# Second attention's entrance and lap in another order, final product by tile, weight splits in two halves

## The chip, the cores and the metric

One core of a Trainium2 chip runs the whole program in one launch. The time is that of the device for one execution, in microseconds (us). TensorE (PE) multiplies, VectorE (DVE), ScalarE (ACT) and GpSimd (POOL) work on elements, and SP issues the DMAs.

## The reference, cut to what matters

512 tokens of width 1024 pass through two blocks of two layers each, all in float32.

- First block, each layer: an RMS norm, three branches (a gated MLP with mixing over 128-token chunks, a retention branch, a gated delta rule), gates, an output product, and a sum onto x. After both layers there is a final norm.
- Second block, each layer: `h = rmsnorm(x)`, then a mixer with 8 self heads (latent attention in the first layer, grouped-query attention with rotary in the second), beside an attention with 4 heads over 256 memory tokens. Then:

```python
mem_out = _memory_attention(q_mem, mem_n, w_mem_kv[i], memq_norm[i], memk_norm[i])
x = x + jnp.concatenate([mix, mem_out], axis=-1) @ w_out[i]
x = x + _swiglu(_rmsnorm(x, norm_ffn[i]), w_gate_up[i], w_down[i])
```

Queries and keys get an RMS norm for each head (and rotary in the self heads) before `softmax(q k^T * scale) v`. The hidden width of the SwiGLU is 2816, that is 22 tiles of 128.

## The kernel before, in words

**Data.** x lies feature-major, xT[128, 8, 512]: eight tiles of 128 features by 512 tokens. Each engine has its own program, written out by hand, and semaphores join them (a wait names a count).

**Weights.** They come as 384 granules of 128x1024 float32 (512 KB) through four slots. For each granule SP loads `raw` (L753); ScalarE casts it to the high part `wh` (`hi2`, L1902, and its like at L1671, L1855, L2216), which waits for `loaded` and for `granule_done`; GpSimd subtracts, `wl = raw - wh` (`split`, L2263 and L2264), and counts `lo_ready`. TensorE waits for `lo_ready` and does three products for each tile (`three`, L822 to L824): high by high, high by low, low by high. Activations are split the same way: for the norm's output `ht` (a ring of four), VectorE scales (`scale_x`, L2924), ScalarE casts `hh` (`scaled_hi`, L1927), GpSimd subtracts `hl` (`scaled_lo`, L2396). `cast(name, parts)` in the attention casts the granules that lie four further on in the slots of those of `name`: "mk" fills those of mv, "mv" those of qm, "qm" of kv, "kv" of qA, "qA" of qB, and "qB" the first four of w_out.

**The second block's attention.** Products come in the order mk, mv (the memory's keys and values, from the split memory tokens mh and ml), then qm, kv, qA, qB from h. While mk and mv are multiplied, the norm of x is made: `square_b` (ScalarE, L1935), `add_b` (VectorE, L2931), and the sum on TensorE behind mv. `attention_block(i)` of each engine holds its own list. Then come steps of heads. Phase 0 has four memory heads, phase 1 eight self heads; each head has four steps, one for each 128 queries, and each phase a few more for what trails. In a step TensorE does QK of one tile (L1482 for the memory, L1487), transposes an earlier P (L1505), and every fourth step PV (L1523). VectorE finds the maximum (L3107) and the bias (L3109), ScalarE the exponential (L2198), VectorE the reciprocal (L3128) and scales P (L3130). The transposed P is copied to mPT, PT or PT_odd by ScalarE (L2187) and VectorE (L3119), the output by ScalarE to mixh (L2206) and by VectorE to mixl (L3136).

`attention_order(i, phases)` (L442) gives the order of steps. In the second attention (i = 1) both phases are one list: the last four steps of phase 0, (0,16) to (0,19), alternate with the first four of phase 1. Between steps each engine has a hook. There ScalarE squares the query tiles of qB (L1983 to L1995), takes roots (L2014), copies the turned queries (`feature`, L2030) and casts granules; VectorE ropes tiles (L2950, L2953, L2957), finishes reciprocals (`finish`, L2847) and does `square_sums` (L2900); TensorE turns query tiles feature-major (`turn_one`, L1338), those of qA at (0,4) to (0,7), those of qB at (1,4) to (1,7) (`late_turns`, L1441). In the phase 1 steps near its end `mixer_early` begins w_out.

**SwiGLU.** 44 granules of up and gate, then 22 of down (`down`, L1595 to L1612). Each down granule is multiplied into all eight output tiles, kt by kt, eight PSUM banks at once. After the last one VectorE adds the eight tiles onto xT in DOWN_ORDER = 4, 5, 6, 7, 0, 1, 2, 3 (L3157), and behind each add of the last layer SP stores the tile (256 KB, L814).

**The first block.** The same granules and splits. VectorE's steps named in the text: gmlp's product y (L2585), retention's rope sum (L2605) and its normalisation (L2634), the convolution (L2701). GpSimd also scales tokens (`scale_tokens`, L2415).

## Time and profile before

| | us |
|---|---|
| median of 3 runs (lowest to highest) | 2765.1 (2763.65 to 2766.12) |
| the profiled execution, its own time | 2765.28 |
| its span | 2763.2 |
| busy: PE | 2666.6 (97%) |
| busy: POOL | 1295.4 (47%) |
| busy: DVE | 1150.4 (42%) |
| busy: ACT | 1140.9 (41%) |
| share of the chain that ended last: PE, DVE, issue, POOL | 83%, 9%, 4%, 2% |

The span is what the profiler recorded of one execution; the 2.1 us between it and that execution's own time lie around the recorded instructions. Busy time says how full an engine is over all stages; it does not say which engine a stage waits for. The waits and the timelines do. A line number such as L2264 is that of the kernel; names such as wl<-raw,wh are the output and the inputs; in brackets stands how long the engine was idle before and what released it. Where a group has "x4", its time is that of four instructions together.

### The profile page before, as it was taken

The numbers are of one execution on the slowest core, as the hardware profiler recorded it, in microseconds if no ns is written. First come the engines' busy times: TensorE is split into PE (matmuls) and PEld (weight loads), VectorE is DVE, ScalarE is ACT, GpSimd is POOL, SyncE is SP. The second block draws the span as 40 slices with busy tenths as digits, with TensorE's granted clock in tenths as the row PEclk, the third lists the DMA queues.
The fourth block names the chain that finished last, engine by engine and source line by source line (L and its number), as shares of the span: only waits on it lengthen the run. The fifth ranks groups of instructions, "written<-read, shape, count | busy, mean of one in ns | idle before, by whom it ended". The sixth has DMA issues, their size and how long they took to land.

```text
span 2763.2 us, 37205 instructions
## 1 busy us (share of the span) xinstructions
PE 2666.6 (97%) x13032; PEld 2162.6 (78%) x13032; DVE 1150.4 (42%) x2191; ACT 1140.9 (41%) x1731; POOL 1295.4 (47%) x672
## 2 busy tenths in 40 slices
PE   7999999999999999999999999999999979999998
PEld 6768898888876888888887648888887746888887
DVE  4677643224477764322466562211104466221100
ACT  5427444323543744432445643333215454333321
POOL 5313565556631366555664213555547311365542
PEclk9999999999999999999999999999999999999999
DMA  4212101233221210133332002333333200233232
GB/s 173 84 45 70 46 26 40 96 99 130 87 79 44 69 40 31 47 99 93 120 115 69 24 31 71 98 98 98 99 109 107 82 31 16 84 106 99 91 99 69
DMA packets 62348, 215.07 MB, mean 78 GB/s; under 512 B 7296, under 2 KB 10496, under 8 KB 61824
## 3 DMA queue, kind: packets, MB, share of 16 engines
q1 hardware_dynamic: 62208, 213.28, 24.5%
q8 instruction: 79, 1.29, 0.2%
q14 instruction: 61, 0.50, 0.1%
HBM read 211.16 MB, written 2.10 MB: 77 GB/s over the span
## 4 chain that ended last, share of the span: by engine, by line
PE 83%; DVE 9%; issue 4%; POOL 2%; ACT 1%; DMA 0%; DVEq 0%; POOLq 0%; SPq 0%; ACTq 0%
PE bank L822 21%; PE bank L824 21%; PE bank L823 20%; PE pair L1523 3%; PE pair L822 2%; PE pair L824 2%; PE pair L823 2%; PE bank L1505 1%; PE bank L989 1%; PE bank L1484 1%; PE bank L1485 1%; DVE pair L2687 1%; DVE prod L2686 1%; PE pair L1338 1%; POOL EG L2341 1%
## 5 line engine op out<-in xcount | busy, mean ns | idle before, releaser
L2264 POOL TENSOR_TENSOR wl<-raw,wh 128x1024 fp32r<-128x1024 f32 x384 | 946.9, 2470 | 1281.7 <-ACT wh L1902 407.8
L822 PE MATMUL bank<-hh,wh 128*128 128x512 f32 x1536 | 607.4, 395 | 3.7 <-DVE y L2774 2.3
L824 PE MATMUL bank<-hh,wl 128*128 128x512 f32 x1536 | 599.2, 390 | 0.0
L823 PE MATMUL bank<-hl,wh 128*128 128x512 f32 x1536 | 598.9, 390 | 0.0
L822 PEld LDWEIGHTS bank<-hh,wh 128*128 128x128 f32 x1536 | 289.3, 188 | 66.2 <-issue 5.5
L823 PEld LDWEIGHTS bank<-hl,wh 128*128 128x128 f32 x1536 | 289.3, 188 | 61.9 <-issue 2.9
L824 PEld LDWEIGHTS bank<-hh,wl 128*128 128x128 f32 x1536 | 288.9, 188 | 60.9
L2216 ACT CAST wh<-raw 128x1024 fp32r<-128x1024 f32 x120 | 125.5, 1048 | 254.0 <-PE pair L824 140.2
L822 PE MATMUL bank<-wh,hh 128*128 128x512 f32 (+2 forms) x352 | 140.7, 400 | 13.1 <-POOL wl L2264 12.5
L1902 ACT CAST wh<-raw 128x1024 fp32r<-128x1024 f32 x84 | 86.7, 1048 | 125.2 <-PE bank L824 105.8
L824 PE MATMUL bank<-wh,hl 128*128 128x512 f32 (+2 forms) x352 | 135.1, 384 | 0.0
L823 PE MATMUL bank<-wl,hh 128*128 128x512 f32 (+2 forms) x352 | 135.0, 383 | 0.0
L2787 DVE TENSOR_TENSOR gs<-gs,bank 128x512 f32<-128x512 f32 x24 | 16.4, 684 | 275.3 <-PE bank L824 275.3
L1671 ACT CAST wh<-raw 128x1024 fp32r<-128x1024 f32 x104 | 108.9, 1049 | 42.7 <-DMA raw<-stream 18.5
L3150 DVE TENSOR_TENSOR at<-row,bank 128x512 f32<-128x512 f32 x44 | 30.3, 688 | 202.2 <-PE bank L824 199.4
L1855 ACT CAST wh<-raw 128x1024 fp32r<-128x1024 f32 x72 | 75.2, 1045 | 85.5 <-PE pair L824 43.8
L822 PE MATMUL bank<-ah,wh 128*128 (+1 forms) x264 | 102.7, 389 | 0.0
L823 PE MATMUL bank<-al,wh 128*128 (+1 forms) x264 | 102.7, 389 | 0.0
L824 PE MATMUL bank<-ah,wl 128*128 (+1 forms) x264 | 102.7, 389 | 0.0
L3147 DVE TENSOR_TENSOR at<-row,bank 128x512 f32<-128x512 f32 x44 | 30.3, 688 | 162.3 <-PE bank L824 161.6
L1871 ACT ACTIVATE gs<-bank 128x512 f32<-128x512 f32 x48 | 28.8, 600 | 166.5 <-PE bank L824 166.5
L822 PEld LDWEIGHTS bank<-wh,hh 128*128 128x128 f32 x352 | 67.8, 193 | 25.4 <-issue 13.8
(462 smaller groups left out, 5314.3 us busy)
## 6 DMA issues: line engine op xcount, KB each, us to landing
raw<-stream SPq DMA_DIRECT2D x384, 512.0 KB, 3.6
mraw<-memin SPq DMA_DIRECT2D x3, 1024.0 KB, 5.6
par<-params SPq DMA_DIRECT2D x2, 1124.5 KB, 9.0
out<-xT SPq DMA_DIRECT2D x8, 256.0 KB, 2.4
con<-consts SPq DMA_DIRECT2D x1, 1540.0 KB, 15.6
xT<-xin SPq DMA_DIRECT2D x1, 1536.0 KB, 8.5
xT<-xin SPq DMA_DIRECT2D x1, 512.0 KB, 3.9
con<-consts SPq DMA_DIRECT2D x1, 512.0 KB, 3.1
```

The lines of the kernel that those rows point to most:

```text
L822: mm(o, ah, bh, start=start, stop=False)
L823: mm(o, ah, bl, start=False, stop=False)
L824: return mm(o, al, bh, start=False, stop=stop)
L1523: x = mm(bk[value_bank(i, phase, a)], vv, pts[a % 2][kb][:, :], start=(kb == 0), stop=(kb == nk - 1))
L1671: nc.scalar.copy(wh[g % SLOTS][:, :], raw[g % SLOTS][:, :]).then_inc(hi_ready, 1)
L1855: nc.scalar.copy(wh[g % SLOTS][:, :], raw[g % SLOTS][:, :]).then_inc(hi_ready, 1)
L1871: A(gs[e][:, :], bk[e], ACT.Sigmoid).then_inc(s["gate_taken"].sem, 1)
L1902: nc.scalar.copy(wh[g % SLOTS][:, :], raw[g % SLOTS][:, :]).then_inc(hi_ready, 1)
L2216: nc.scalar.copy(wh[slot][:, :], raw[slot][:, :]).then_inc(hi_ready, 1)
L2264: return TT(wl[slot][:, :], raw[slot][:, :], wh[slot][:, :].bitcast(F32), ALU.subtract)
L3147: V.tensor_tensor(at_[j][:, :], row[:, :], bk[2 * j], ALU.mult).then_inc(t["f_gate"].sem, 1)
L3150: V.tensor_tensor(at_[j][:, :], row[:, :], bk[2 * j + 1], ALU.mult).then_inc(t["f_up"].sem, 1)
```

## The change

Five things are edited; what is computed stays the same.

1. **Entrance of the second attention.** ScalarE's casts of "mk", its scaled_hi, squares and casts of "mv" come in another order; so do GpSimd's splits and scaled_lo, and VectorE's scale_x and add_b.
2. **The lap.** TensorE keeps its order (PE_LAP). ScalarE and VectorE go through the eight steps in SOFTMAX_LAP. The turns of qB stand at steps 4, 6, 8, 9 of phase 1 instead of 4, 5, 6, 7. ScalarE copies qB's last tile to a new buffer `qraw`; VectorE ropes it from there at (1,2), not at (0,17), and TensorE's first transpose of phase 1 no longer waits for that tile. `finish` moves from (0,16) to (0,18).
3. **Casts of "qB"** (w_out's first four granules) move from (0,16) to (0,19) to steps 12, 16, 20, 24 of phase 1.
4. **The last down product.** Its granules 20 and 21 are done tile by tile, six matmuls for each tile; `granule_done` is counted for each tile, and VectorE's add waits for its own tile.
5. **Every split** of a granule on GpSimd is two subtractions of 128x512, the count given by the second.

```diff
@@ -353,6 +353,7 @@
...
 QUERY_TURNS = ((("qA", 0), ("qA", 1)), (("qA", 2), ("qA", 3)), (("qpe0", 0), ("qpe0", 1)), ())
+QB_TURNS = (4, 6, 8, 9)
 FILL_STEPS = (0, 1, 2, 3, 4, 6, 8, 10, 12, 14, 16, 18)
@@ -439,15 +440,18 @@
-def attention_order(i, phases):
+PE_LAP = ((0, 16), (1, 0), (0, 17), (1, 1), (0, 18), (1, 2), (0, 19), (1, 3))
+SOFTMAX_LAP = ((0, 16), (0, 17), (0, 18), (1, 0), (1, 1), (1, 2), (0, 19), (1, 3))
+def attention_order(i, phases, lap):
...
     first, second = rows[0], rows[1]
-    lap = len(first) - 16
-    return first[:16] + [r for two in zip(first[16:], second[:lap]) for r in two] + second[lap:]
+    return first[:16] + [rows[p][x] for p, x in lap] + second[4:]
@@ -654,6 +658,7 @@
...
             b["PT_odd"] = tiles_at("PT_odd", 4, hreg)
+            b["qraw"] = sb("qraw", [P, T], at=hreg + 24 * KB_)
     ah = sb("ah", [P, FF, T], F32R, at=r1)
@@ -1438,7 +1443,7 @@
...
-                    late_turns = {(0, 4 + x): ("qA", x) for x in range(4)} | {(1, 4 + x): ("qB", x) for x in range(4)}
+                    late_turns = {(0, 4 + x): ("qA", x) for x in range(4)} | {(1, y): ("qB", x) for x, y in enumerate(QB_TURNS)}
@@ -1459,7 +1464,7 @@
...
                 outs = O_BANKS[i]
-                for phase, step, now, turn, values, _ in attention_order(i, phases):
+                for phase, step, now, turn, values, _ in attention_order(i, phases, PE_LAP):
                     m0, a0 = (0, 0) if phase == 0 else (16, 4)
@@ -1494,6 +1499,8 @@
...
                                 n = count_before(ROPED[i], group[phase]) + dict(ROPED[i])[group[phase]]
+                                if len(phases) == 2 and phase:
+                                    n -= 1
                                 pe.wait_ge(t["roped"].sem, t["roped"].at(n))
@@ -1608,8 +1615,18 @@
...
                         down(a * 4 + (d0 + 2 + j), a * 4 + (2 + j), (d0 + 2 + j) % SLOTS, False, False)
-                for kt in range(18, FF):
+                last = FF if i == 0 else FF - 2
+                for kt in range(18, last):
                     down(d0 + kt, kt, (d0 + kt) % SLOTS, False, kt == FF - 1)
+                if i == 1:
+                    pe.wait_ge(lo_ready, d0 + FF)
+                    pe.wait_ge(t["f_lo"].sem, t["f_lo"].at(FF + 2))
+                    for e in DOWN_ORDER:
+                        for kt in range(FF - 2, FF):
+                            slot = (d0 + kt) % SLOTS
+                            c = slice(e * P, (e + 1) * P)
+                            o = three(bk[e], wh[slot][:, c], wl[slot][:, c], ah[:, kt], al[:, kt], False, kt == FF - 1)
+                        o.then_inc(granule_done, 1)
@@ -1992,6 +2009,8 @@
...
                         m = A(b["v"][x][:, :], p[:, 256:512], ACT.Copy)
+                    if (i, name, x) == (1, "qB", NT - 1):
+                        m = A(b["qraw"][:, :], p, ACT.Copy)
                     m.then_inc(t["evac"].sem, 1)
@@ -2115,21 +2134,25 @@
...
                 else:
-                    cast("mk", [0])
+                    cast("mk", [0, 1])
                     for k in range(2):
                         scaled_hi(k)
-                    cast("mk", [1])
-                    for k in range(2, KD):
+                    cast("mk", [2])
+                    for k in range(2, 4):
                         scaled_hi(k)
+                    for n in range(2):
+                        square_b(n)
+                    cast("mk", [3])
                     take(to_token, "mk")
-                    cast("mk", [2, 3])
-                    for n in range(4):
-                        square_b(n)
+                    square_b(2)
+                    scaled_hi(4)
                     cast("mv", [0])
-                    for n in range(4, 6):
-                        square_b(n)
+                    scaled_hi(5)
+                    square_b(3)
+                    for k in range(6, KD):
+                        scaled_hi(k)
                     cast("mv", [1])
-                    for n in range(6, KD):
+                    for n in range(4, KD):
                         square_b(n)
@@ -2159,10 +2182,10 @@
...
                                 take_root("qB")
-                            if 16 <= step:
-                                cast("qB", [step - 16])
-                        elif 5 <= step < 9:
-                            feature("qB", step - 5, bk[6])
+                        elif step in QB_TURNS:
+                            feature("qB", QB_TURNS.index(step), bk[6])
+                        elif step in (12, 16, 20, 24):
+                            cast("qB", [step // 4 - 3])
@@ -2170,7 +2193,7 @@
...
                     act.wait_ge(t["mix_lo"].sem, t["mix_lo"].at(4))
-                for phase, step, now, turn, _, outputs in attention_order(i, phases):
+                for phase, step, now, turn, _, outputs in attention_order(i, phases, SOFTMAX_LAP):
                     m0, a0 = (0, 0) if phase == 0 else (16, 4)
@@ -2261,7 +2284,9 @@
             def split(slot):
-                return TT(wl[slot][:, :], raw[slot][:, :], wh[slot][:, :].bitcast(F32), ALU.subtract)
+                for c in (slice(0, GB * P // 2), slice(GB * P // 2, GB * P)):
+                    m = TT(wl[slot][:, c], raw[slot][:, c], wh[slot][:, c].bitcast(F32), ALU.subtract)
+                return m
@@ -2436,10 +2461,10 @@
...
                 else:
-                    split_granules("mk", [0, 1])
+                    split_granules("mk", [0, 1, 2])
                     for k in range(4):
                         scaled_lo(k)
-                    split_granules("mk", [2, 3])
+                    split_granules("mk", [3])
                     split_granules("mv", [0])
@@ -2961,6 +2986,8 @@
...
                     p = bk[GROUPS[i][name].banks[x]][:, 0:heads * dim]
+                    if (i, name, x) == (1, "qB", NT - 1):
+                        p = b["qraw"][:, :]
                     rope(p, tab, x, heads, dim, dst[:, x, 0:heads * dim])
@@ -2985,9 +3012,16 @@
...
                     own(V.memset(bk[7], 1.0))
-                    for n in range(KD):
-                        scale_x(n)
-                for n in range(1, KD):
+                    for k in range(4):
+                        scale_x(k)
+                    add_b(1)
+                    for k in range(4, 6):
+                        scale_x(k)
+                    add_b(2)
+                    scale_x(6)
+                    add_b(3)
+                    scale_x(7)
+                for n in range(4 if i else 1, KD):
                     add_b(n)
@@ -3071,6 +3105,9 @@
                         if phase:
+                            if step == 2:
+                                rope_tile("qB", NT - 1, 4, P, b["tab"][0:2], tok[TOK[i]["qB"]])
+                                own.end()
                             return
@@ -3080,19 +3117,18 @@
...
                             count["root"] -= 1
+                        if step == 18:
                             finish("qA")
                             finish("qB")
-                        if step % 4 == 1 and step > 4:
+                        if step in (5, 9, 13):
                             rope_tile("qB", step // 4 - 1, 4, P, b["tab"][0:2], tok[TOK[i]["qB"]])
-                            if step == 17:
-                                own.end()
...
                 last_now = {}
-                for phase, step, now, turn, _, outputs in attention_order(i, phases):
+                for phase, step, now, turn, _, outputs in attention_order(i, phases, SOFTMAX_LAP):
                     m0, a0 = (0, 0) if phase == 0 else (16, 4)
@@ -3152,8 +3188,8 @@
...
                     memory_sum(1, 2)
-                for e in DOWN_ORDER:
-                    dve.wait_ge(granule_done, g0 + G_UP + FF)
+                for n, e in enumerate(DOWN_ORDER):
+                    dve.wait_ge(granule_done, g0 + G_UP + (FF if i == 0 else FF - 1 + n))
                     V.tensor_tensor(xT[:, e], xT[:, e], bk[e], ALU.add).then_inc(s["x_ready"].sem, 1)
```

## Rows read from the trace of the kernel before

**Rows 1.** The page, busy time of each engine, and the group of the weight splits.
```profile
PE 2666.6 (97%) x13032; PEld 2162.6 (78%) x13032; DVE 1150.4 (42%) x2191; ACT 1140.9 (41%) x1731; POOL 1295.4 (47%) x672
...
L2264 POOL TENSOR_TENSOR wl<-raw,wh 128x1024 fp32r<-128x1024 f32 x384 | 946.9, 2470 | 1281.7 <-ACT wh L1902 407.8
```

**Rows 2.** The waits of TensorE: us in total, times, longest us.
```profile
PE bank L822 <- POOL wl L2264: 16.9, 2, 12.5
...
PE pair L1523 <- ACT mPT L2187: 10.2, 2, 9.2
...
PE bank L959 <- DVE y L2585: 2.5, 2, 1.3
```

**Rows 3.** Windows: us, busy PE, PEld, DVE, ACT, POOL, then PEclk, DMA, GB/s.
```profile
2109.00:2116.00 7.00, 5.39 (x12) 3.88 (x13) 5.03 (x7) 6.13 (x11) 7.00 (x4) 0.51 0.42 129
...
2242.00:2252.50 10.50, 5.81 (x10) 2.61 (x11) 6.56 (x13) 5.40 (x9) 7.01 (x3) 0.51 0.38 130
...
2285.00:2320.00 35.00, 35.00 (x130) 18.25 (x129) 29.15 (x78) 20.49 (x44) 0.00 (x0) 1.00 0.00 1
...
2758.00:2761.00 3.00, 0.00 (x0) 0.00 (x0) 2.16 (x4) 0.00 (x0) 0.00 (x0) 0.50 1.03 383
```

**Rows 4.** TensorE's timeline, entrance of the second attention: start us, us, what.
```profile
2110.61 0.79 PE L822 MATMUL bank<-wh,mh 128*128 128x512 f32 x1 [4.47 <-POOL wl L2264]
...
2116.01 0.40 PE L822 MATMUL bank<-wh,mh 128*128 128x512 f32 x1
...
2118.53 0.39 PE L824 MATMUL bank<-wh,ml 128*128 128x512 f32 x1
```

**Rows 5.** GpSimd's timeline at the entrance.
```profile
2099.65 5.05 POOL L2396 TENSOR_TENSOR hl<-ht,hh 128x512 fp32r<-128x512 f32 x4
...
2108.20 7.51 POOL L2264 TENSOR_TENSOR wl<-raw,wh 128x1024 fp32r<-128x1024 f32 x3 [3.50 <-ACT wh L1902]
```

**Rows 6.** VectorE's timeline at the entrance.
```profile
2101.04 0.75 DVE L2924 SCALAR_TENSOR_TENSOR ht<-xT,gain,pair 128x512 f32<-128x512 f32 x1 [4.12 <-POOL hl L2396]
```

**Rows 7.** VectorE's timeline in the lap of the two phases.
```profile
2238.75 2.14 DVE L3109 SCALAR_TENSOR_TENSOR soft<-soft,rn 128x1 f32<-128x1 f32 x1
```

**Rows 8.** ScalarE's timeline in the lap.
```profile
2235.90 1.28 ACT L2014 ACT_TABLE_LOAD   x1
```

**Rows 9.** TensorE's timeline in the lap.
```profile
2246.69 3.78 PE L1523 MATMUL pair<-mPT,mv 128*128 128x512 f32 x4 [9.24 <-ACT mPT L2187]
...
2257.72 0.66 PE L1338 MATMUL pair<-con,tok 128*128 128x128 f32 x4 [1.93 <-ACT q L2030]
...
2262.28 0.86 PE L1338 MATMUL pair<-con,tok 128*128 128x128 f32 x4 [2.60 <-ACT q L2030]
...
2267.22 0.66 PE L1338 MATMUL pair<-con,tok 128*128 128x128 f32 x4 [1.52 <-ACT q L2030]
```

**Rows 10.** VectorE's timeline, the gmlp branch of the first layer.
```profile
109.84 2.87 DVE L2585 TENSOR_TENSOR y<-gm_t,ug 128x512 f32<-128x512 f32 x1
...
113.47 0.69 DVE L2585 TENSOR_TENSOR y<-gm_t,ug 128x512 f32<-128x512 f32 x1
```

**Rows 11.** GpSimd's timeline, four short products in a row, first attention.
```profile
1489.96 4.10 POOL L2415 TENSOR_TENSOR tok<-tok,rn 128x512 f32<-128x512 f32 x4 [3.77 <-DVE rn L2847]
```

**Rows 12.** VectorE's timeline at the same time.
```profile
1490.37 0.64 DVE L3109 SCALAR_TENSOR_TENSOR soft<-soft,rn 128x1 f32<-128x1 f32 x1
```

**Rows 13.** VectorE's timeline, phase 0 of the second attention.
```profile
2195.83 1.81 DVE L3130 TENSOR_SCALAR mP<-mP,soft 128x256 f32<-128x256 f32 x1
...
2200.48 0.35 DVE L3130 TENSOR_SCALAR mP<-mP,soft 128x256 f32<-128x256 f32 x1
```

**Rows 14.** VectorE's timeline, the end of the kernel.
```profile
2755.28 1.28 DVE L3157 TENSOR_TENSOR xT<-xT,bank 128x512 f32<-128x512 f32 x2 [118.17 <-PE pair L824]
...
2757.68 2.48 DVE L3157 TENSOR_TENSOR xT<-xT,bank 128x512 f32<-128x512 f32 x4
```

**Rows 15.** SP's timeline, the end of the kernel.
```profile
2756.00 4.52 SPq L814 DMA_DIRECT2D out<-xT  x8
```

## The prediction

> **What bounds the kernel now.** I read the shares of the engines first. TensorE is busy 2666.6 us of a span of 2763.2 [rows 1], so an edit can win only the 97 us in which TensorE stands still, the stretches in which it runs at its lower clock, and the tail. Next the waits of TensorE [rows 2]: three answer to this change. The wait for a weight's low part has a longest of 12.5 us (the start of the kernel) and a second of 16.9 - 12.5 = 4.4; the wait for mPT has one of 9.2; that for the gmlp's y is 1.3 in each of two layers. Then the timelines around the 4.4 and the 9.2, engine by engine, to see what each waiting engine had in its queue. Last the clock in windows: it is 0.51 of full (the 1.2 GHz level) right behind both waits, and 1.00 (2.4 GHz) in the steady part of the second attention, where TensorE has no gap at all [rows 3].
>
> The profiled execution took 2765.28 with its launch, the median of three is 2765.1: I sum against 2765.3. 0.2% is 5.5 us, about what a measurement of this kernel can tell from no change.
>
> **Entrance of the second attention.** The mv product stops for 4.47 at 2110.61 until its third weight's low part is there; then 12 matmuls take 5.40 (2110.61 to 2116.01), where the next 12 take 2.74 (2.52 for eleven starts, to 2118.53, and one more) [rows 4]. Why is that split late? GpSimd stands idle 3.50 and then does three splits in 7.51 [rows 5]. It waited for the cast of "mk", 2 on ScalarE (a cast refills its slot for the granule four further on, here mv's third), which stands in ScalarE's order behind six hh casts (k = 2 to 7) and the mk tokens; the hh casts wait for ht, and ht (a ring of four) waits 4.12 for GpSimd's own hl [rows 6]. The change puts casts and splits of mk's granules 1 and 2 ahead of most of that. GpSimd's queue is then: split 1 at 2096.3 to 2098.8, four hl to be cut by split 2 (cast at 2099.3, done 2102.8), hl until 2107.9 (5.05 for four, [rows 5]), split 3 until 2110.4. TensorE has the third granule in time, does half of it (6 matmuls, 1.36) and stands from 2107.2 to 2110.4: an idle of 3.2 for 4.47. From there 18 matmuls at full clock end at 2114.5 instead of 2118.75, a gain of 4.25 (bound above). The idle is still long, and after each one of 4.4 and 9.2 the clock stood at 0.51; so I let half the slow matmuls come back, 2 us, and take **-2.3**, bound below -1.3. The squares and add_b, moved forward, lie beside the product (VectorE stands idle 4.12 there, [rows 6]); if that cover went, ssb would be late by one add of 0.7.
>
> **Lap of the two phases.** TensorE's order stays, ScalarE's and VectorE's changes. Now the copy of the last memory head's mPT stands behind (1,0) and (1,1): a reduce, a bias that takes 2.14 because a split holds the port [rows 7], rope of the last qB tile, a table load of 1.28 for sqrt [rows 8] and one like it for exp. After: the copy follows the roots at once, at about 2238.0 instead of 2246. The sqrt load and the qraw copy (0.5) remain ahead of it. TensorE's PV starts at 2238.75, an idle of 1.3 for 9.24 [rows 9]. What is late next: the first P of the second phase (idle 2.4, since exp's table comes after mPT), the PT copies (1.9), the last q feature (0.9). Today the four idles are 9.24 + 1.93 + 2.60 + 1.52 = 15.29 [rows 9]; then 1.3 + 2.4 + 1.9 + 0.9 = 6.5: 8.8 less. Today two stretches here run at 0.51. The first has 5.81 us of busy TensorE [rows 3], which at 1.00 would be 2.9; the second begins at 2262.28, where a turn takes 0.86 for 0.66 [rows 9], and costs an estimated 1.5. With the long idle gone I take 3.2 of these 4.4 as gained: **-12.0**, bounds -8 (the clock as today, and one idle more) and -14 (clock up throughout, two of the small idles half as long).
>
> The four casts of w_out go to steps 12 to 24. There TensorE and VectorE run 35.00 and 29.15 of 35 us [rows 3], so VectorE has 5.85 free in 35, 0.7 for each pair of steps of 4.33, and a half split can hold a VectorE op for 1.1. Four splits are eight halves, one pair in each fourth step: most of it is absorbed by the steps between; I take **+0.6**, bounds 0 and +3. SP's loads into these four slots are released 30 to 50 us later; the granules they bring are cast after the last steps of the phase, over 25 us later still, and a load takes 3.6, so that is covered. Turning qB at steps 4, 6, 8, 9 delays heads 4 to 7 only.
>
> **Splits in halves.** 384 splits of 2.47 [rows 1]. The nearest row of 128x512 is hl, 5.05 for four, 1.26 each [rows 5]: two are 2.52, some +0.12 against a split alone (2.39). In the products TensorE uses a granule in 5.44, so this lies beside it. What halves can buy is the port: y takes 2.87 where a split holds the port and 0.69 alone [rows 10], and TensorE waits for y 1.3 in each layer [rows 2]. With the port let go between halves the stall is 1.0 shorter on average; four GpSimd ops in a row (4.10) let VectorE's bias in after 0.64 [rows 11, 12], so letting in works. For two layers I take y 1.15 and small ones nothing: **-2.3**, bounds +2 and -6 (y in [rows 10] and the P scaling in [rows 13] are two of 23 such stalls on the chain of waits; 1.1 each at best, and a quarter of them stand before something late). In phase 0 of the second attention the P scaling takes 1.81, and 0.35 alone [rows 13], and a gap of 0.97 on TensorE follows from it: **-0.8**. At the start the first split ends 0.12 later and so does ssum: **+0.2**.
>
> By the rows the halves cost GpSimd nothing when VectorE gets in between: four ops took 1.03 each with three VectorE ops let in between [rows 11, 12], and no longer than that. The Trainium skill, SBUF — State Buffer, Who interferes with whom, says that whoever issues first has the shared pair for the whole instruction and the other fully blocks. By it the second half would wait for the VectorE op let in (0.7), on the one awaited split: 2745 instead of 2744.
>
> **Last product by tile.** Today the eight final adds follow the product, the last four over 2.48, to 2760.16, and SP's eight stores are issued over 4.52 [rows 14, 15] and move 383 GB/s [rows 3], 2.1 MB in 5.5 us: store-bound. After, a tile ends every 6 matmuls, 1.36; an add (0.69), an issue and a transfer of 0.69 fit inside that. Behind the last matmul only one add, issue, transfer and landing remain: 0.69 + 0.85 (from the add's end to moving data) + 0.69 + 0.9 (from the last data to the span's end) = 3.1, say 3.2, where 2763.2 - 2755.3 = 7.9 stands now: **-4.7**. TensorE waits for both last granules together; the last split is done at 2737, needed at 2744. Bounds -3.5 (landing slower) and -5.3.
>
> **Sum.** -2.3 - 12.0 + 0.6 - 2.3 - 0.8 + 0.2 - 4.7 = -21.3: 2765.3 - 21.3 = 2744.0.
>
> ScalarE has two table switches in the lap. The row shows 1.28 for the load [rows 8] and the root starts 0.02 behind it. The Trainium skill, ScalarE: Activation LUTs, What ACT_TABLE_LOAD costs, has 1.38 of drain besides, 2.66 a switch. With that before both, mPT and the first P would come 1.4 to 2.6 later and the time would be 2746; no gap of that size stands in front of the load here.
>
> **Rivals.**
> - *The clock stays up and halves are worth their bound*: entrance -4.25, lap -14, halves -5. 2765.3 - 29 = 2737. For it: the idle in the entrance is shorter than both that were followed by 0.51. Against: 3.2 is nearer to 4.4 than to the steady part. 0.17.
> - *The lap's wait only moves*: the PV comes early, but the first P, rope of qB's last tile (2.1 on VectorE, now in (1,2)) and PT copies queue behind one another, so the idles sum to 13, and the clock falls as today; the lap gives 5. 2744 + 7 = 2751. For it: VectorE is as full as before, and work was only permuted. 0.20.
> - *Halves cost where VectorE is full*: each locked op alternates with a half instead of waiting once, +0.12 on each of some 100 splits beside VectorE-bound work, 13: 2757. Against: a stage where VectorE is that full has few splits now, and a half lets go of the port sooner. 0.09.
> - *Slower*: GpSimd's splits become what TensorE waits for, in every product; 384 x 0.12 = 46, less the 21: 2790. It decides only if a granule's cast plus split exceeds its 5.44 of TensorE, and it is 1.05 + 2.52. 0.03.
> - *The parts do nothing*, as the entrance and lap waits are inferred from the wrong releaser, leaving 3 to 5 of the tail: 2761. 0.03.
>
> The forecast itself, 2740 to 2748, has 0.48. The range 2735 to 2753 takes in it, the first two rivals and the bounds. Faster by over 0.2% (below 2759.8): 0.48 + 0.17 + 0.20 + 0.09 = 0.94; within 0.03; slower 0.03.
>
> **What would show it.** Entrance: the mv product's idle is 3 us or less and sits between its granule 2 and 3. Lap: PE's wait for mPT is under 2, the first lap PV starts some 8 us earlier after the last QK before it, and new waits for P and PT of about 2 each appear. Halves: 768 splits of about 1.25, y at about 1.7, wait for y near 0. Tail: span ends 3.2 behind the last matmul. I am wrong if TensorE's waits for P or q in the lap exceed 8, if steps 12 to 24 show gaps, or if GpSimd's splits appear among TensorE's waits in the products.

## The result and the profile after

| | before | changed |
|---|---|---|
| median of 4 runs each, us (lowest to highest) | 2764.76 (2763.65 to 2766.12) | 2740.46 (2737.67 to 2743.19) |
| the profiled execution, its span | 2763.2 | 2738.6 |

The ratio is 0.9911, with a 95% interval of 0.9897 to 0.9924: 24.3 us faster. The forecast was 2744.0 in a range of 2735 to 2753.

The page of the changed kernel, busy time and the group of the splits (now L2288), which answer to [rows 1]:

```profile
PE 2660.0 (97%) x13032; PEld 2158.2 (79%) x13032; DVE 1084.0 (40%) x2191; ACT 1139.7 (42%) x1732; POOL 1384.8 (51%) x1056
...
L2288 POOL TENSOR_TENSOR wl<-raw,wh 128x512 fp32r<-128x512 f32 x768 | 1036.3, 1373 | 1175.5 <-ACT wh L1919 380.8
```

VectorE is busy 66 us less than before with the same 2191 instructions: that is time that it had stood blocked inside instructions while GpSimd split; "the port" below means this (in the three profiled kernels with whole splits it is busy 1149 to 1150, in e1, which changes the splits alone, 1084.9). GpSimd is busy 89 us more. TensorE is busy 6.6 us less with the same matmuls, so of the 24.6 us of span 6.6 are put down to the clock and 18.0 are time in which TensorE stood still (in the tail too).

The waits of TensorE (columns as in [rows 2]):

```profile
PE bank L827 <- POOL wl L2288: 16.0, 2, 12.4
PE bank L1512 <- DVE PT L3155: 3.4, 3, 1.3
...
PE bank L1512 <- DVE PT_odd L3155: 2.2, 2, 1.1
PE pair L1530 <- ACT mPT L2210: 2.1, 2, 1.2
PE pair L1343 <- DVE tok L2982: 2.0, 1, 2.0
...
PE bank L964 <- DVE y L2610: 0.4, 2, 0.2
```

The second wait for a weight's low part is 16.0 - 12.4 = 3.6, where it was 4.4. The 9.2 for mPT is 1.2, the two of 1.3 for y are 0.2. New are 2.0 for tok and several of 1.1 for PT and PT_odd. The entrance, TensorE and then GpSimd, beside [rows 4, 5]:

```profile
2102.56 0.50 PE L827 MATMUL bank<-wh,mh 128*128 128x512 f32 x1 [3.57 <-POOL wl L2288]
```

```profile
2094.56 5.50 POOL L2421 TENSOR_TENSOR hl<-ht,hh 128x512 fp32r<-128x512 f32 x4
2100.00 5.00 POOL L2288 TENSOR_TENSOR wl<-raw,wh 128x512 fp32r<-128x512 f32 x4
```

GpSimd still does four hl before mv's last split, 2100.00 to 2102.5. The lap, TensorE and then ScalarE, beside [rows 8, 9]:

```profile
2227.61 1.98 PE L1530 MATMUL pair<-mPT,mv 128*128 128x512 f32 x4 [1.17 <-ACT mPT L2210]
...
2234.67 0.63 PE L1343 MATMUL pair<-con,tok 128*128 128x128 f32 x4 [2.02 <-DVE tok L2982]
...
2240.99 0.63 PE L1512 MATMUL bank<-con,P 128*128 128x128 f32 x4 [1.28 <-DVE PT L3155]
...
2245.07 0.65 PE L1343 MATMUL pair<-con,tok 128*128 128x128 f32 x4 [0.41 <-ACT q L2049]
```

```profile
2225.37 1.28 ACT L2033 ACT_TABLE_LOAD   x1
2226.66 0.32 ACT L2033 ACTIVATE sdv<-rn 128x16 f32<-128x16 f32 x2
2226.89 0.67 ACT L2210 ACTIVATE mPT<-bank,rn 128x512 f32<-128x512 f32 x1
2227.58 1.28 ACT L2221 ACT_TABLE_LOAD   x1
2228.87 0.78 ACT L2221 ACTIVATE P<-bank,soft,rn 128x512 f32<-128x512 f32 x1
```

The four idles are 1.17 + 2.02 + 1.28 + 0.41 = 4.9, where 15.3 stood. The second is not one of the first P (TensorE waited 0.20 for that, at 2229.79): it stands before the first turn of qB, which needs the rope of qB's last tile. Steps 12 to 24, TensorE at the first of the moved casts, and the window over all four (columns as in [rows 3]):

```profile
2259.21 0.63 PE L1512 MATMUL bank<-con,P 128*128 128x128 f32 x4 [0.99 <-DVE PT L3155]
```

```profile
2253.00:2290.00 37.00, 32.69 (x121) 16.75 (x120) 29.41 (x69) 21.88 (x44) 9.98 (x8) 1.00 0.18 57
```

And the tail, VectorE's last add and SP's stores, beside [rows 14, 15]:

```profile
2735.46 0.69 DVE L3193 TENSOR_TENSOR xT<-xT,bank 128x512 f32<-128x512 f32 x1 [0.67 <-PE bank L829]
```

```profile
2726.66 9.85 SPq L819 DMA_DIRECT2D out<-xT  x8
```

The last matmul ends at 2735.4, the span at 2738.6: 3.2 where 7.9 stood. The stores are issued over 9.85 as the tiles come.

**Where the 24.6 us came from.** TensorE's order is the same in both kernels but for qB's turns and the last two granules, so the start of one and the same matmul can be compared in the two traces. At the mk product of the second attention (2089.54 and then 2081.03) 8.5 are won; at the first QK of phase 0, 10.1; before the lap, 11.0; at the first PV of phase 1 (2271.61 and 2246.86), 24.75; after step 24, 19.8; at the end 24.6.

| step | forecast | measured |
|---|---|---|
| start, first block and first attention (halves) | -2.1 | -8.5 |
| entrance of the second attention | -2.3 | -1.6 |
| phase 0 | -0.8 | -1.0 |
| lap | -12.0 | -13.7 |
| four splits in steps 12 to 24 | +0.6 | +4.9 |
| tail | -4.7 | -4.8 |

These are readings of one execution each. For most rows other kernels with the same code in the stage agree: phase 0 gave 1.0 in e1 and 0.0 in e2 and e8, whose splits are whole; the lap gave 13.4 to 13.8 in all ten kernels that have both its new order and the moved casts; behind the last matmul stand 8.0 us in e1 and e8, which have the old tail, and 3.2 in all others. The first row is different. Up to the mk product of the second attention ten of the profiled kernels (the changed one, e1, e3 to e7, e10 to e12) have the same code, and there they had won 8.5, 12.7, 12.4, 11.0, 10.6, 11.6, 10.4, 10.5, 7.7 and 3.1; before, e2 and e8, with whole splits, stood at 0, -2.4 and -1.2. So the -8.5 is one draw out of 3.1 to 12.7, with a mean of 9.8.

### The profile page after: what moved, and what is told of

The parts are those of the page before. It is cut to its first block, busy times and chain, and to the rows that moved or that the text cites. A ratio compares the mean times of both kernels' runs of the same rounds, so it can differ in the third digit from the quotient of the medians.

```text
span 2738.6 us, 37589 instructions
## 1 busy us (share of the span) xinstructions
PE 2660.0 (97%) x13032; PEld 2158.2 (79%) x13032; DVE 1084.0 (40%) x2191; ACT 1139.7 (42%) x1732; POOL 1384.8 (51%) x1056
## 3 DMA queue, kind: packets, MB, share of 16 engines
q1 hardware_dynamic: 62208, 213.28, 24.3%
## 4 chain that ended last, share of the span: by engine, by line
PE 82%; DVE 9%; issue 4%; POOL 2%; ACT 1%; DMA 0%; POOLq 0%; DVEq 0%; SPq 0%; ACTq 0%
PE bank L827 21%; PE bank L829 21%; PE bank L828 21%; PE pair L827 2%; PE pair L829 2%; PE pair L828 2%; PE pair L1530 2%; PE bank L994 1%; PE bank L1489 1%; PE bank L1490 1%; PE bank L1512 1%; DVE pair L2712 1%; DVE prod L2711 1%; POOL EG L2366 1%; PE pair L1343 1%
## 5 line engine op out<-in xcount | busy, mean ns | idle before, releaser
L2288 POOL TENSOR_TENSOR wl<-raw,wh 128x512 fp32r<-128x512 f32 x768 | 1036.3, 1373 | 1175.5 <-ACT wh L1919 380.8
L827 PE MATMUL bank<-wh,hh 128*128 128x512 f32 (+2 forms) x352 | 140.6, 399 | 13.8 <-POOL wl L2288 12.4
```

What stands on the lines that cost most here:

```text
L827: mm(o, ah, bh, start=start, stop=False)
L2288: m = TT(wl[slot][:, c], raw[slot][:, c], wh[slot][:, c].bitcast(F32), ALU.subtract)
```

## The experiments

Twelve kernels, each timed beside the kernel before. "Won" below is read at one and the same matmul in the profiled executions, as above.

| run | median | before | ratio, 95% interval |
|---|---|---|---|
| e1_halves_alone | 2754.6 | 2766.0 | 0.9966 (0.9953 to 0.9978) |
| e2_whole_splits | 2748.9 | 2766.0 | 0.9936 (0.9922 to 0.9949) |
| e3_cast_behind_mixh | 2741.7 | 2766.0 | 0.9915 (0.9901 to 0.9928) |
| e4_casts_in_lap | 2741.1 | 2766.0 | 0.9914 (0.9900 to 0.9928) |
| e5_fill_gap | 2737.9 | 2766.5 | 0.9901 (0.9886 to 0.9916) |
| e6_split_earlier | 2741.1 | 2766.5 | 0.9915 (0.9901 to 0.9928) |
| e7_casts_step11 | 2737.3 | 2766.5 | 0.9897 (0.9882 to 0.9912) |
| e8_casts_moved_alone | 2767.8 | 2766.5 | 1.0005 (0.9996 to 1.0014) |
| e9_quarters | 2737.2 | 2767.1 | 0.9894 (0.9878 to 0.9911) |
| e10_reordered | 2736.5 | 2767.1 | 0.9893 (0.9877 to 0.9910) |
| e11_filled | 2733.6 | 2767.1 | 0.9880 (0.9864 to 0.9897) |
| e12_whole_where_in_a_row | 2735.3 | 2767.5 | 0.9885 (0.9869 to 0.9902) |

The intervals of e3 to e7, e9, e10 and e12 overlap that of the changed kernel (0.9897 to 0.9924), and e11's ends where it begins. So no median alone tells these kernels from the changed one; what an edit did is read in the stage where it was made.

**Halves: e1 and e2.** e1 is the kernel before with this alone:

```diff
-                return TT(wl[slot][:, :], raw[slot][:, :], wh[slot][:, :].bitcast(F32), ALU.subtract)
+                for c in (slice(0, GB * P // 2), slice(GB * P // 2, GB * P)):
+                    m = TT(wl[slot][:, c], raw[slot][:, c], wh[slot][:, c].bitcast(F32), ALU.subtract)
+                return m
```

> The kernel before with the halved splits and nothing else. Theory A (letting VectorE in between the halves shortens TensorE's idles, and where an idle gets short enough the granted clock stays at 1.00 behind it): the first block's product after its two layers starts 8.5 us earlier, as in the changed kernel, half of it idle and half clock; phase 0 of the second attention gives 1 more, and the lap, whose bias waits 2.14 for a split, some 1 to 2. Total about -10 to -12: 2753 to 2755. Theory B (the gain of the first block is worth only the idle, about 4, and the rest was the luck of one execution): 2759 to 2761. Theory C (halves cost where VectorE is full): over 2765.

Its waits of TensorE:

```profile
PE pair L1523 <- ACT mPT L2187: 8.7, 2, 7.8
...
PE pair L978 <- DVE rt L2604: 2.8, 2, 1.4
...
PE bank L1129 <- DVE Y L2760: 2.5, 8, 0.3
```

It won 11.4 by the medians, 13.5 by the profile at the end of the first block, and 1.0 in phase 0. In the entrance, where the old order stands, it lost 0.6, and in the lap 1.0: the wait for mPT is 7.8, shorter, but the clock was low for 20.5 us there. The wait for rt (4.5 in the kernel before, 2.3 a time) is 2.8. So theory A holds for the first block, not for the lap. e2 is the changed kernel with the opposite edit.

> The changed kernel with each split as one subtraction again. Theory A: it loses the first block's 8.5 and phase 0's 1, and the four splits in steps 12 to 24 hold the bias for up to 2.2 in place of 0.6, so these steps lose some 6 more than the 4.9 of the changed kernel; the entrance, whose third split starts behind four hl either way, stays. 2740.5 + 8.5 + 1 + 6 = 2756. Theory B (first block worth 4, steps as now): 2746.

```profile
PE bank L845 <- DVE qT L2676: 5.1, 2, 2.5
PE pair L983 <- DVE rt L2625: 4.5, 2, 2.3
...
PE bank L964 <- DVE y L2608: 2.5, 2, 1.3
```

The waits for qT, rt and y are back. It is 17.1 faster than before, the changed kernel 24.3: the halves are worth 7 there, against 11.4 in e1, two numbers that these intervals (some 3.5 us either way for each kernel) don't tell apart. Its entrance won 1.5 with whole splits, so the new order alone makes that gain. The median, 2748.9, lies nearer theory B's 2746. Its steps 12 to 24 lost 4.4 in all, less than the 4.9 with halves. There theory A, which had added 6 for them, fell: a whole split costs as little as two halves, so it isn't the length of one GpSimd instruction that counts in these steps.

**The moved casts: e3, e7, e4, e8.** e3 puts ScalarE's hook of phase 1 behind the copy to mixh:

```diff
-                    if (i, phase) == (1, 1):
-                        late(phase, step)
                     for o in outputs:
...
+                    if (i, phase) == (1, 1):
+                        late(phase, step)
```

> The changed kernel with ScalarE's hook of phase 1 behind the copy to mixh instead of ahead of it, so that the four casts of steps 12, 16, 20, 24 no longer stand ahead of mixh. In the changed kernel each of these steps costs TensorE 1.25. Theory A (0.7 of it is the cast of 1.05 that delays mixh, and so mixl and all behind it on VectorE, 0.6 is the bias held by a half split): each costs 0.6, total -2.7, 2738. Theory B (all of it is the port): no change, 1.1 to 1.25 for each remain. Theory C (all of it is the cast): the four waits vanish, -4.9.

VectorE and TensorE at the first of these steps:

```profile
2251.15 0.94 DVE L3145 SCALAR_TENSOR_TENSOR soft<-soft,rn 128x1 f32<-128x1 f32 x1
...
2252.20 1.39 DVE L3166 TENSOR_SCALAR P<-P,soft 128x512 f32<-128x512 f32 x1
```

```profile
2255.86 0.63 PE L1512 MATMUL bank<-con,P 128*128 128x128 f32 x4 [1.52 <-DVE PT L3155]
```

Each step now cost more, 1.7, or 6.7 in all. The split starts 0.3 behind the end of mixl and holds the bias (0.94 for 0.16) and the scaling of P (1.39 for 0.49). None of the three theories had this: the cast in front of mixh was not the cost, and behind it the split falls wholly on instructions of VectorE that the port can hold up. The median, 2741.7, doesn't show the loss; the trace does. e7 goes the other way:

```diff
-                        elif step in (12, 16, 20, 24):
-                            cast("qB", [step // 4 - 3])
+                        elif step in (11, 15, 19, 23):
+                            cast("qB", [(step - 11) // 4])
```

> The changed kernel with the four casts of w_out's granules at steps 11, 15, 19, 23 instead of 12, 16, 20, 24. Theory A (the loss of 1.25 at each is the port, held while VectorE has locked work, and VectorE waits 1.1 to 1.8 for mixh in each head: a split that starts 1.4 earlier lies in that wait): each costs 0.7 or less, at least 2.2 us come back, 2738. Theory B (a split costs VectorE the same wherever it lies, as whole and half splits and two places so far gave 1.1 to 1.7): -19.8 at the end of the attention stays within 0.5.

```profile
2250.61 2.50 POOL L2288 TENSOR_TENSOR wl<-raw,wh 128x512 fp32r<-128x512 f32 x2 [64.66 <-ACT wh L1919]
```

```profile
2250.19 0.49 DVE L3166 TENSOR_SCALAR P<-P,soft 128x512 f32<-128x512 f32 x1
2251.89 0.69 DVE L3172 TENSOR_TENSOR mixl<-pair,mixh 128x512 fp32r<-128x512 f32 x1 [1.21 <-ACT mixh L2229]
```

The split lies at 2250.61 to 2253.1, begins as VectorE ends its scaling of P, and the first half is over while VectorE waits 1.21 for mixh; the second lies beside mixl, which reads one of its inputs from PSUM (pair) and took 0.69 as it does elsewhere. TensorE has no idle in these steps; 4.9 became 0.2, here and in e10, e11 and e12. Theory A, and more than it asked for. By the medians it is 29.1 below before, where the changed kernel was 24.3.

e4 leaves the casts in the lap, at (0,16) to (0,19), in the new order.

> The changed kernel with the four casts of w_out's first granules back at (0,16) to (0,19) as in the kernel before, in the new order of steps. Theory A (they were moved because in the lap ScalarE's queue and the port are on TensorE's path: casts of 1.05 ahead of the exponentials, splits over bias, over the rope whose inputs now both lie in SBUF): the lap loses 4 to 8 and steps 12 to 24 win 4.9 back: between -1 and +3. Theory B (the lap's gain comes from the order alone): -4.9, 2735.5.

```profile
2227.02 3.68 PE L1530 MATMUL pair<-mPT,mv 128*128 128x512 f32 x4 [3.08 <-ACT mPT L2210]
...
2238.39 1.09 PE L1343 MATMUL pair<-con,tok 128*128 128x128 f32 x4 [4.25 <-DVE tok L2982]
```

```profile
2225.51 7.64 POOL L2288 TENSOR_TENSOR wl<-raw,wh 128x512 fp32r<-128x512 f32 x6 [40.25 <-ACT wh L1919]
```

```profile
2233.95 2.88 DVE L2978 TENSOR_TENSOR rb<-qraw,tab 128x256 f32<-128x256 f32 x2
```

The lap won 6.1 instead of 13.7, and the steps lost nothing: 7.6 against 4.9, theory A. Part of the 7.6 is clock: it was low for 10.2 us in this lap, in two stretches. Rope, which reads two tiles in SBUF since it reads qraw, takes 2.88 for 0.75 beside a split; TensorE waits 4.25 for it. e8 is the other half, the casts moved in the kernel before:

> The kernel before with only the four casts moved from the lap to steps 12, 16, 20, 24, splits whole. From the runs so far: the lap is worth 13.7 with order and casts, 6.1 with the order alone. Theory A (the two add up): the casts alone give 7.6 in the lap, and cost 4.4 in the steps: -3.2, 2762. Theory B (the old order hides it, since mPT waits for the bias and the rope of (1,0) and (1,1) anyway, and only their stalls of 2.0 and 1.4 go): the lap gives 3.4 to 4.5 and the steps take it back: within 1 of 2765, and the two parts of the change need each other.

```profile
2244.43 3.78 PE L1523 MATMUL pair<-mPT,mv 128*128 128x512 f32 x4 [5.90 <-ACT mPT L2187]
```

The wait for mPT fell from 9.24 to 5.90, but with the clock low over three stretches there the lap won only 1.7, and the steps lost 4.4. 6.1 + 1.7 is not 13.7: order and casts need each other, theory B (though it had 3.4 to 4.5 for the lap). The casts alone gave no gain.

**Entrance and clock: e5, e6.** e5 puts matmuls into the idle:

```diff
+                        if (i, name, q, x) == (1, "mv", n - 1, 0):
+                            down_taken(2)(0)
+                            for _ in range(12):
+                                mm(bk[2], b["mh"][:, 0, 0:P], wh[(g - 1) % SLOTS][:, 0:T], start=True, stop=True)
```

> The changed kernel with 12 more matmuls (products of operands already there, into a bank that the next product overwrites) ahead of TensorE's wait for the last mv weight, where it stands idle 3.57 and the clock then is 0.50 for 3.4 us. Theory A (the clock falls because of the idle, and its fall costs half of the stretch): the 12 take 2.7 of the idle, the product's end is not delayed by them, the clock stays 1.00, and the qm product starts 1.4 to 1.7 earlier: 2739. Theory B (the clock behind the entrance has nothing to do with this idle): the stretch at 0.50 stays and the time is the same, or 0.5 longer.

```profile
2100.51 0.50 PE L827 MATMUL bank<-wh,mh 128*128 128x512 f32 x1 [0.91 <-POOL wl L2292]
```

```profile
2100.50:2110.00 9.50, 9.49 (x50) 8.14 (x51) 6.05 (x25) 6.74 (x11) 9.50 (x8) 1.00 0.34 110
```

```profile
2103.00:2106.00 3.00, 3.00 (x10) 2.31 (x9) 2.32 (x4) 2.49 (x5) 3.00 (x3) 0.55 0.45 175
```

With 0.91 of idle left the clock is 1.00 behind it (second fence), where the changed kernel had 0.55 (third). The entrance won 3.4 instead of 1.6. Theory A. It isn't chance: in the changed kernel, e3, e4 and e7, with the same idle unfilled, the clock was low for 3.4 us behind it each time; in e5 and e11, where it is filled, it stayed at 1.00 there both times. e6 attacks the idle itself, with GpSimd's split of granule 3 behind two scaled_lo:

> The changed kernel with GpSimd's split of mk's granule 3 behind two scaled_lo instead of four. The split now starts at 2100.00, five us after its cast. Theory A (the idle is GpSimd's queue): it starts 2.5 earlier, the idle goes from 3.57 to about 1.1, behind which the clock stays up: 2.5 idle and 1.5 clock, the qm product 4.0 earlier, 2736.5. Theory B (what is moved behind it becomes late: hl 2 and 3, so ht 6 and 7, hh, and the sums and the first qm products): the gain is under 1.

```profile
2097.01 0.50 PE L827 MATMUL bank<-wh,mh 128*128 128x512 f32 x1 [1.10 <-POOL wl L2288]
...
2105.72 1.19 PE L1380 MATMUL pair<-con,gain 128*128 128x128 f32 x4 [4.33 <-DVE ssb L2958]
```

The first idle is 1.10 as theory A had it, and a new one of 4.33 stands before the statistics: the sum of squares is queued on VectorE behind ht 6 and 7, which now wait for hl 2 and 3. From within it the clock was low for 10.2 us. The entrance lost 2.2 against the changed kernel's 1.6 won. Theory B, and stronger.

**Smaller pieces, and the best orders: e9 to e12.**

> The changed kernel with each split as four subtractions of 128x256 instead of two of 128x512. Theory A (VectorE's stall is what is left of the GpSimd instruction that holds the port, so it halves again, and a granule's split has slack everywhere but at the entrance): in the first layer the four idles that follow such stalls (2.8, 1.4, 1.3 and 1.0) shrink by 0.3 to 0.6 each, and the clock stays up in more of them; the steps 12 to 24 stay at 1.1 each, as whole and half splits gave about the same there; the entrance loses 0.3. Between -1 and -4: 2737 to 2740. Theory B (each piece costs 0.12 and a new alternation with VectorE's locked work): +1 to +3, 2742 to 2744.

```profile
PE 2663.6 (97%) x13032; PEld 2161.5 (79%) x13032; DVE 1056.7 (39%) x2191; ACT 1140.0 (42%) x1732; POOL 1510.4 (55%) x1824
```

Quarters took another 27 us from VectorE's busy time and put 126 on GpSimd. The first layer's idles before rt and at the sums went from 1.4 to 1.0 and from 2.8 to 1.5, but the first product began 0.8 later (13.26 for 12.44); the idles in steps 12 to 24 stayed at 0.95 to 1.07, 4.8 lost in all. The profiled execution is the slowest of its four (2743.11), and in it the entrance lost 1.7 where the changed kernel won 1.6: the step on mom that e10 shows below took 5.67 through eight quarters, and TensorE's turn of mk came 1.98 late. The median is 29.9 below before's (theory A), though the interval overlaps that of the changed kernel.

e10 has e6 and e7, and the squares 4 to 7 and their additions ahead of tiles 6 and 7.

> The changed kernel with the casts of w_out at steps 11, 15, 19, 23, the split of mk's granule 3 behind two scaled_lo, and the squares 4 to 7 with their additions ahead of the scaling and casting of tiles 6 and 7. The early split alone took the idle in the mv product from 3.57 to 1.10, and made a new one of 4.33 before the statistics, since the sum of squares stood behind ht 6. Theory A (that order is all that made it late): the sum is there 4 earlier, the second idle is under 0.5, the clock stays 1.00; the entrance gives 5.5 instead of 1.6, the steps 4.7: 2740.5 - 3.9 - 4.7 = 2732. Theory B (the qm product then waits for its own first weight or hl): the entrance gives 2.5: 2735.

The idle of 4.33 was 0.49, and at the start of qm the entrance had won 5.2, near theory A's 5.5. Then 3.6 of it were given back: 1.5 as the clock fell for 3.4 us after all, behind idles of only 1.12 and 0.49, and the rest on VectorE, GpSimd and TensorE:

```profile
2107.80 7.66 DVE L2906 SCALAR_TENSOR_TENSOR rn<-mom 128x8 f32<-128x8 f32 x1
2115.50 0.17 DVE L2907 SCALAR_TENSOR_TENSOR rn<-mom,rn 128x8 f32<-128x8 f32 x1
```

```profile
2107.91 7.53 POOL L2287 TENSOR_TENSOR wl<-raw,wh 128x512 fp32r<-128x512 f32 x6
```

```profile
2122.62 0.44 PE L1343 MATMUL pair<-con,tok 128*128 128x128 f32 x2 [2.37 <-POOL tok L2439]
```

One step of VectorE of 128x8 (a statistic, on the tile mom), 0.17 alone, took 7.66: it stood blocked through six half splits in a row, and TensorE's turn of mk, which follows from it, came 2.37 late. The changed kernel has the same in small: this step (L2905 there) took 4.36, the turn came 0.69 late, and in e3, e4 and e7 it was the same within 0.05. e1 and e5 didn't: the same step took 1.18 and 0.98, and VectorE got in behind each half. The median, 2736.5, is nearer theory B's 2735, but what theory B had named, a wait of qm, isn't what took the gain.

> The changed kernel with the casts at steps 11, 15, 19, 23 and the 12 filling matmuls in the entrance's idle. They lie in different stretches, so they add: 2740.5 - 1.6 - 4.7 = 2734. If the clock of one stretch depended on more than the idle right before it, the sum would be off by over 1.

The medians add: 33.5 below before, the lowest of all. The profiled execution was the slowest of its four (2737.97); in it the step on mom took 5.97, and the entrance lost what the fill had won. Its entrance has the same code as e5's, so this difference is one of the execution; nor is it where the step falls in a half, for it began 0.33 behind the start of one in e5 and 0.34 in e11. e12 tried to avoid it, with those three splits whole:

> The reordered kernel (e10) with four filling matmuls in the idle of 1.1 that it left in the mv product, and with mv's three splits that GpSimd does in a row (qm's last three granules) whole instead of in six halves. In e10 VectorE's step on mom took 7.66 there: it was shut out through six halves, and TensorE's first turn of mk came 2.37 late; with whole splits two runs so far showed 1.9 and 2.5. Theory A (between two GpSimd instructions that follow at once VectorE is let in often but not always, and more pieces in a row give more chances to be passed over, where a whole split is over in 2.4 and a wait comes first more often): the step takes under 2.6, the turn's idle is under 1.2, the entrance gives 3.5 to 5 instead of 1.6: 2736.5 - 2.5 = 2734. Theory B (it is chance, or the phase in which VectorE comes, and has nothing to do with the number of pieces): the step takes 4 to 8 again, and the time stays at 2736.

```profile
2115.25 0.23 DVE L2912 SCALAR_TENSOR_TENSOR rn<-mom 128x8 f32<-128x8 f32 x1
2115.51 2.32 DVE L2913 SCALAR_TENSOR_TENSOR rn<-mom,rn 128x8 f32<-128x8 f32 x1
2117.87 2.32 DVE L2923 SCALAR_TENSOR_TENSOR rn<-em,rn 128x8 f32<-128x8 f32 x1
...
2120.30 2.24 DVE L3097 SCALAR_TENSOR_TENSOR e<-e,con 128x4 f32<-128x4 f32 x1
```

```profile
2129.02 0.55 PE L1347 MATMUL pair<-con,tok 128*128 128x128 f32 x2 [2.69 <-POOL tok L2444]
```

VectorE was let in behind each whole split, as theory A had it, but it has three such steps in a row, and each waited for a whole split. They took the same 7, and the turn came 2.69 late, so the entrance kept 1.1 of the 5.2 won at qm. By time it is no better than e10. How often VectorE is passed over, and by what, stays open.

## Why the prediction was right, and where its sizes were off

**Sum and sign.** 2744.0 against 2740.5. The sign, the stages and what waits in them held, but for one wait of the lap. That the sum came within 3.5 us is luck in part: the first row came out 6.4 better than forecast and the moved splits 4.3 worse, and the first row alone differs by up to 9.6 us between executions of the same code.

**Halves.** The step "for two layers I take y 1.15 and small ones nothing" failed. The idles per layer fell by 1.08 for y, 0.86 for rt, 0.6 for rqT and 1.5 for qT (tiles of VectorE that TensorE waits for): 4.1 a layer, not 1.15. I set the others to nothing without looking for what each stood in front of, and the result lies outside the bound of -6 that I had given the term. New idles took back 2.4: 0.5 in each layer (LM, GpSimd's own chain), 0.8 at the second layer's first product and 0.6 at the first attention's. In the ten executions with this code TensorE stood still 33.6 to 35.8 us between its first matmul and that attention, and 40.1 to 42.2 in the three with whole splits: some 6 us that every execution shows. The rest is the clock, and that varies: it was low for 3.4 to 23.9 us in the ten, 17.1 to 20.5 in the three. In the changed kernel TensorE's busy time until the branches of the second layer are done went from 1096.3 to 1093.7. e1 shows the halves alone. My reason, the port let go between halves, is what the rows show: y took 1.79 and 0.92 in place of 2.87 and 0.69, and 66 us of VectorE's busy time are gone. The rival that halves cost 13 where VectorE is full is refuted by e1. The rival with the halves at -5 adds up to -28.0 and not to -29; its 2737 is right.

**Moved splits.** The step "most of it is absorbed by the steps between" failed: +0.6 was +4.9, beyond the bound of +3, and of the signs of being wrong this one came true: steps 12 to 24 show gaps, four of 0.99 to 1.11. VectorE has free time in the mean, but TensorE's transposes of P wait for its order step by step; each split cost 1.1 to 1.25 whether whole or halved (e2), 1.7 when it began later (e3), and nothing when it began 1.4 earlier, into VectorE's wait for mixh (e7). It was a matter of place, not of size.

**Lap.** -12.0 was -13.7. mPT and PV came as worked out (idle 1.17 for 1.3), and the clock was 1.00 throughout. Of the later idles those for PT and the last q feature were 1.28 and 0.41 for 1.9 and 0.9, but "the first P of the second phase (idle 2.4, since exp's table comes after mPT)" was wrong: TensorE waited 0.20 for P. In its place stood 2.02 for the rope of qB's last tile, which I had named in a rival and not in the sum; that the sizes are alike is luck. What I had in one term was two that need each other: the order alone gives 6.1 (e4), the casts alone 1.7 (e8).

**Entrance.** The idle was 3.57 for my 3.2, and for the "3 us or less" of my own signs, as the split ended 0.6 later than worked out; the clock fell as I let it, and 1.9 was won at qm; 0.3 went again at the turn of mk, behind the step of 4.36. The rival "the clock stays up" was right for the lap and wrong here.

**Tail and phase 0.** -4.8 for -4.7, -1.0 for -0.8. ScalarE's two switches took 1.28 each, begun 0.02 behind the instruction before and with the next 0.01 behind them (the lines at 2225.37 and 2227.58), so the 1.38 of drain that the Trainium skill, ScalarE: Activation LUTs, What ACT_TABLE_LOAD costs, adds is not seen here, and the trace decides.

## What to carry to other kernels

Where two engines share a port, ask not only how long the blocking instruction is but where it lies against the other engine's own waits: moving four casts by one step won 4.7 us in these steps, which neither halving nor delaying them did. Cutting a blocking instruction in two is worth its small overhead where the other engine has lone steps on the path, and is a gamble where many pieces follow in a row. An idle of the tensor engine is paid twice when the clock falls behind it, so filling one with matmuls that compute nothing can win as much as a reordering does: 1.8 us here in e5, though e11's profiled execution lost it again behind the blocked step.

## What the runs showed that was not expected

- VectorE is not always let in between two GpSimd instructions that follow at once: steps of 0.17 took 4.36, 5.97 and 7.66, through up to six half splits, in some kernels and executions, and 0.98 to 1.2 in others. The Trainium skill, SBUF — State Buffer, Who interferes with whom, has the pair held for the whole instruction; these rows show a loser that waits through several. My price of that rule (1 us on one split) looked at the wrong engine.
- Where the clock falls differs between executions of nearly the same code. The changed kernel and e3 have the same first block. The changed kernel's clock was low at 881.4 to 888.2 and e3's was not, and at the end of that block they had won 9.4 and 13.3. A single execution can't price a clock effect of 3 us. The window of either, the changed kernel first:

```profile
880.00:888.00 8.00, 7.84 (x29) 6.40 (x28) 5.53 (x6) 2.90 (x5) 2.69 (x2) 0.58 0.22 66
```

```profile
880.00:888.00 8.00, 7.84 (x46) 6.68 (x45) 5.33 (x6) 3.27 (x5) 2.70 (x2) 1.00 0.21 66
```

- In the profiled executions the clock was low for 44.4 us before the tail in the kernel before, 37.4 of them busy, and for 20.5 in the changed one, all of them busy. That is 16.9 busy us less at half the clock, by which I estimate 8.5 us; TensorE's busy time fell by 6.6. What makes the difference wasn't looked into.
